# mLSTM layer with modulated norms: input projection in two passes over its rows, attention spread over the V and O strips

## The reference, cut to what matters

```
sh1, sc1, g1, sh2, sc2, g2 = split(silu(c) @ w_mod + b_mod, 6)       # w_mod 2048 x 12288
hm = rms_norm(x) * (1 + sc1) + sh1
q, k, v, o, g = split(hm @ w_in)                                     # 1024, 1024, 2048, 2048, 16 columns
h  = causal mLSTM of q, k, v with gates from g; per-head rms_norm * h_norm
x  = x + g1 * ((sigmoid(o) * h) @ w_out)
hf = rms_norm(x) * (1 + sc2) + sh2
x  = x + g2 * (conv_ffn(hf, w_up, conv, w_down))
```

## Time and profile before

| | us |
|---|---|
| median of 3 runs (1316.69 to 1318.73) | 1316.71 |
| span of the profiled execution, first to last instruction | 1314.5 |
| PE busy in it | 1190.8 (91%) |
| DVE busy | 942.9 (72%) |
| ACT busy | 552.2 (42%) |
| POOL busy | 202.8 (15%) |

### The profile page before, as it was taken

The page is one execution under the profiler, slowest core; times in us unless marked ns, Lnnn a source line. Parts: engine busy times, 40 slices in busy tenths (PEclk is TensorE's granted clock), DMA queues, the critical chain, the costliest instruction groups (busy, mean ns, idle before and its releaser), DMA issues.

```text
span 1314.5 us, 22606 instructions
## 1 busy us (share of the span) xinstructions
PE 1190.8 (91%) x8034; PEld 1104.8 (84%) x8034; DVE 942.9 (72%) x916; ACT 552.2 (42%) x711; POOL 202.8 (15%) x182
## 2 busy tenths in 40 slices
PE   0128998999999999499999999999999999999998
PEld 0127887999999888499999888999999888999986
DVE  7889883666667699779888756667666556776763
ACT  0315445444444444444444433444444434444432
POOL 0040000011010121212211112122111112222221
PEclk9958999999999999699999999999999999999999
DMA  8997997788687599759999556666665656666562
GB/s 360 422 401 284 407 362 203 199 246 226 192 236 246 195 364 369 221 166 270 271 283 286 193 194 194 189 178 175 189 191 177 204 190 179 181 186 175 179 197 90
DMA packets 303757, 311.24 MB, mean 237 GB/s; under 512 B 5000, under 2 KB 251208, under 8 KB 291176
## 3 DMA queue, kind: packets, MB, share of 16 engines
q1 hardware_dynamic: 303108, 310.42, 73.6%
q0 software_dynamic: 176, 0.16, 0.1%
q10 hardware_dynamic: 438, 0.19, 0.1%
HBM read 308.66 MB, written 2.10 MB: 236 GB/s over the span
## 4 chain that ended last, share of the span: by engine, by line
PE 86%; DVE 8%; issue 3%; DMA 2%; ACT 1%; POOL 1%; POOLq 0%; DVEq 0%; SPq 0%
PE ps L992 17%; PE ps L994 17%; PE ps L993 17%; PE ps L1012 10%; PE ps L1013 10%; PE ps L1014 10%; DVE acc L778 5%; DMA raw<-in_l_w_mod_dram 2%; PE ps L1021 1%; DVE hm_lo L764 1%; ACT w_hi L488 1%; DVE xnT L760 1%; DVE h_tok L870 1%; PE ps L1128 0%; PE ps L1125 0%
## 5 line engine op out<-in xcount | busy, mean ns | idle before, releaser
L741 DVE TENSOR_TENSOR w_lo<-raw,w_hi 128x1024 fp32r<-128x1024 f32 x392 | 520.0, 1340 | 214.0 <-ACT w_hi L488 214.0
L488 ACT ACTIVATE w_hi<-raw 128x1024 fp32r<-128x1024 f32 x392 | 414.0, 1057 | 400.6 <-PE ps L1014 228.2
L992 PE MATMUL ps<-hm_hi,w_hi 128*128 128x256 f32 x1920 | 546.9, 285 | 11.2 <-DVE hm_lo L764 9.1
L993 PE MATMUL ps<-hm_lo,w_hi 128*128 128x256 f32 x1920 | 544.5, 284 | 0.0
L994 PE MATMUL ps<-hm_hi,w_lo 128*128 128x256 f32 x1920 | 544.5, 284 | 0.0
L992 PEld LDWEIGHTS ps<-hm_hi,w_hi 128*128 128x128 f32 x1920 | 369.9, 193 | 11.6 <-issue 10.0
L993 PEld LDWEIGHTS ps<-hm_lo,w_hi 128*128 128x128 f32 x1920 | 370.0, 193 | 0.1
L994 PEld LDWEIGHTS ps<-hm_hi,w_lo 128*128 128x128 f32 x1920 | 369.8, 193 | 0.0
L753 DVE SCALAR_TENSOR_TENSOR acc<-mod_raw,cT,acc 128x2048 f32<-128x2048 f32 x64 | 151.1, 2362 | 7.7 <-DMA mod_raw<-in_l_w_mod_dram 7.6
L1012 PE MATMUL ps<-w_hi,act_hi 128*128 128x512 f32 x352 | 137.1, 389 | 0.0
L1013 PE MATMUL ps<-w_lo,act_hi 128*128 128x512 f32 x352 | 137.0, 389 | 0.0
(11 more groups left out here) (155 smaller groups left out, 1002.2 us busy)
## 6 DMA issues: line engine op xcount, KB each, us to landing
raw<-in_l_w_up_dram SPq DMA_DIRECT2D x88, 1024.0 KB, 5.8
mod_raw<-in_l_w_mod_dram SPq DMA_DIRECT2D x64, 1024.0 KB, 7.5
raw<-in_l_w_in_dram SPq DMA_DIRECT2D x48, 1024.0 KB, 7.9
raw<-in_l_w_down_dram SPq DMA_DIRECT2D x44, 1024.0 KB, 5.0
raw<-in_l_w_mod_dram SPq DMA_DIRECT2D x32, 1024.0 KB, 7.1
raw<-in_l_w_out_dram SPq DMA_DIRECT2D x16, 1024.0 KB, 7.5
x<-in_x_dram SPq DMA_DIRECT2D x2, 1024.0 KB, 10.0
out_dram<-x SPq DMA_DIRECT2D x8, 256.0 KB, 4.9
```

Source lines behind the costliest of these rows:

```text
L488: nc.scalar.activation(w_hi[:, v % 4, :], raw[:, v // 2 % 4, (v % 2) * HALF:(v % 2 + 1) * HALF], ACT.Copy).then_inc(w_hi_made, 1)
L741: nc.vector.tensor_tensor(w_lo[:, v % 4, :], raw[:, v // 2 % 4, (v % 2) * HALF:(v % 2 + 1) * HALF], w_hi[:, v % 4, :].bitcast(f32), ALU.su ...
L992: mm(out, hi, hm_hi[:, k, :], start=(k == 0), stop=False)
L993: mm(out, hi, hm_lo[:, k, :], start=False, stop=False)
```

## The change

It touches stages 1 to 7 up to the first up unit; the up and down products stay as they are.

**Prefix.** Scale and shift are first made for the first 768 columns only (`K_FIRST` = 6 row tiles). SP loads x and then 16 pieces `m0` of 256 rows x 768 columns, and these are summed by PE itself: `sum_m0` uses each 128x128 block of `m0` as stationary operand and one column of `cT` as the moving one. The remaining 1280 columns (`m1`, 32 pieces of 640 KB) are added up by DVE during the first pass.

**Input projection.** It runs over half units of two row tiles x 512 columns, `in_half`, in 12 strips (V0 to V3, O0 to O3, K0, K1, Q0, Q1). Pass 1 covers the first 6 row tiles (3 halves a strip, 36 in all). ACT stores the partial sums (`store_strip`). Pass 2 covers the other 10 (5 halves a strip, 60 in all): K and Q first, then V and O strips in turn. DVE adds the partial sums (`add_strip`). So K and Q of all heads exist before the attention.

**Attention.** The 40 V and O halves of pass 2 and the 32 halves of the output product are *slots*. In slot e each engine runs its split or its half and then `attend(e)`, which holds the pieces of a head at fixed slots: scores at 5+5h, product with V at 9+5h, transpose at 13+5h. `o_sig` and `gated` are now token-major and `o_lo` is made by DVE. x is overwritten by attention buffers and loaded again before the residual add.

**The other w_mod pieces.** A table, `MOD_SLOT`, gives the half after whose split DVE adds each piece.

```diff
+    K_FIRST = 6
+    PAIRS = (K_FIRST // 2, (KT - K_FIRST) // 2)
...
+    MOD_SLOT = [V_PASS1 + p for p in (6, 7, 9, 11, 12, 14, 16, 17, 19)] \
+        + [V_VO + e for e in (1, 3, 4, 8, 9, 11, 13, 14, 18, 19, 21, 23, 24, 28, 29, 31, 33, 34, 38, 39)] \
+        + [V_OUT + f for f in (3, 6, 8, 9, 11, 12, 13, 15, 17, 18, 19, 20, 21, 22, 23, 25, 27, 29, 30)]
...
+    E_SCORES, E_PV, E_HT, E_HEAD = 5, 9, 13, 5
...
             sp.dma_start(c_rows[:], c_d[0, :].rearrange("(k p) -> k p", p=P)).then_inc(c_in, 16)
-
-            for n in range(2):
-                sp.wait_ge(acc_cleared, n + 1)
...
+            for t in range(TB):
+                sp.dma_start(x[:, t, :], x_d[0, t * P:(t + 1) * P, :]).then_inc(x_in[t], 16)
+            for i in range(16):
+                load_m0(i)
+            for vh in range(6):
+                load_half(vh)
+            for i in range(2 * KT):
+                load_m1(i)
+                load_half(6 + i)
...
+                if r == 10:
+                    sp.wait_ge(hT_ready, H)
+                    for t in range(TB):
+                        sp.dma_start(x[:, t, :], x_d[0, t * P:(t + 1) * P, :]).then_inc(x_in[t], 16)
...
+            def sum_m0(i):
+                n, rt = i // 8, 2 * (i % 8)
+                pe.wait_ge(m0_in[i % 8], 16 * (n + 1))
+                for j in range(2):
+                    for k in range(K_FIRST):
+                        c0 = k * (KT + 1) + rt + j
+                        last = mm(ps[:, M0_BANK[n], c0:c0 + 1],
+                                  m0[:, i % 8, j * M0_COLS + k * P:j * M0_COLS + (k + 1) * P],
+                                  cT[:, rt + j:rt + j + 1], start=True, stop=True)
+                last.then_inc(m0_used, 1)
...
+            for p in range(V_PASS1):
+                in_half(p)
+                if p == 24:
+                    pe.wait_ge(m1_used, KT)
+                    pe.wait_ge(sc0_made, 2)
+                    column_sums(0, 3, 0, KT - K_FIRST)
+                if p == V_PASS1 - 3:
+                    pe.wait_ge(m1_used, 2 * KT)
+                    column_sums(1, 0, 0, KT - K_FIRST)
...
+            for p in range(V_PASS1):
+                split_lo(p + 3)
+                if 1 <= p <= 2 * KT:
+                    add_m1(p - 1)
```

More of the change, by code:

```diff
@@ L458, in _ @@
             rstd_of_x(1)
+            pool.wait_ge(colsum_done, 3)
             clear_acc(5)
@@ L654, in _, with store_strip @@
-            nc.scalar.preload_act_table_set("exp_and_others")
-            with act.Fori(0, H - 1) as h:
-                head(h, False)
-            head(H - 1, True)
-            nc.scalar.preload_act_table_set("silu_and_others")
+                    nc.scalar.activation(out, src, ACT.Copy, bias=1.0).then_inc(sc_made, 1)
+                else:
+                    nc.scalar.activation(out, src, ACT.Copy).then_inc(sc_made, 1)
+            def store_strip(m):
+                for b in range(2):
+                    nc.scalar.activation(strip_sums(0, m)[b], bank_pair(m, b), ACT.Copy)\
+                             .then_inc(evac0, 1)
@@ L661, in squares @@
+            for p in range(V_VO, V_OUT):
+                slot_hi(p)
+                attend(p - V_VO)
             def squares(q):
@@ L883, in _ @@
-            with dve.Fori(0, H - 1) as h:
-                head(h, False)
-            head(H - 1, True)
+            copy_xT(0)
+            for n, out in ((0, scale_p), (1, shift_p)):
+                dve.wait_ge(m0_summed, n + 1)
+                sums = ps[:, M0_BANK[n], 0:K_FIRST * (KT + 1)]
+                nc.vector.reduce_sum(out[:, 0:K_FIRST], sums.rearrange("p (b r) -> p b r", r=KT + 1),
+                                     mybir.AxisListType.X).then_inc(sc0_made if n else sc0_step, 1)
+                if n == 0:
+                    dve.wait_ge(sc0_step, 1)
+                    nc.vector.tensor_scalar(out[:, 0:K_FIRST], out[:, 0:K_FIRST], 1.0, None, ALU.add)\
+                             .then_inc(sc0_made, 1)
@@ L1149, in _ @@
-            with pe.Fori(0, H - 1) as h:
-                head(h, False)
-            head(H - 1, True)
+            for i in range(4, 16):
+                sum_m0(i)
+            for p in range(V_PASS1):
+                in_half(p)
[6 more added lines that the diff above has]
+                    column_sums(1, 0, 0, KT - K_FIRST)
@@ new lines, in _ @@
+            for p in range(V_PASS1, V_VO):
+                in_half(p)
+            pe.wait_ge(wg_made, 4)
+            pe.wait_ge(hm_made, KT)
+            pe.wait_ge(params_made, 3)
+            out = ps[0:F_ROW0 + H, 2, 0:SEQ]
+            for k in range(KT):
+                c0 = k // 8 * 2 * F_ROW0 + k % 8 * H
+                hi, lo = wg_hi[:, c0:c0 + F_ROW0 + H], wg_lo[:, c0:c0 + F_ROW0 + H]
+                mm(out, hi, hm_hi[:, k, :], start=(k == 0), stop=False)
+                mm(out, hi, hm_lo[:, k, :], start=False, stop=False)
+                last = mm(out, lo, hm_hi[:, k, :], start=False, stop=(k == KT - 1))
```

1042 lines of the change are left out of this document (567 added, 475 removed).

## The result

| | before | after |
|---|---|---|
| median of 5 runs each, in turn on one chip | 1318.73 us | 1326.61 us |
| lowest | 1316.69 | 1324.86 |
| profiled execution: span | 1314.5 | 1323.0 (its own time 1324.86) |

The ratio is 1.0063, with a 95% interval of 1.0045 to 1.0081: 0.6% slower. One run of after took 1402.14 us at a granted clock of 0.827, and is left out of the ratio; the others are at 0.954 to 0.956.

A forecast was written before the change was run, and what follows sets the result against it. Before the change: w_mod loads bound the prefix, then PE; after it, DVE sets the pace. Output product ending +10.4 and second norm -3.9 give +6.5 on 1314.5, so 1321; with run offset 1323 us, range 1300 to 1337.

The forecast's parts named there:

- step 1: Prefix: sums on PE at 0.216 us a record, 88.1 us; first half at 105.5 against 106.7, a gain of 1 us.
- Rival B: Prefix: the sums run at the full clock and lose 42 us, giving 1281 us; chance 0.10.
- steps 2 and 3: Pass 1, then K, Q and gates of pass 2: paced by PE, ending at 211.9 and 275.3, DVE's work hidden.
- step 4: V and O strips of pass 2: DVE 17.8 us plus 1.6 lost with ACT, 19.4 a head; slot 39 left at 427.3.
- So the order decides: V and O strips: DVE at 17.8 and PE at 18.2 us a head are level, so waits between engines set the pace.
- step 5: Output product: DVE is the path, 106 us plus 4 for loads, so 110; end at 537.3 where before 526.9.
- step 6: Second norm: both `add_mod` are gone from it, 33.8 - 3.9 = 29.9 us.
- my two gains: Second norm: 1.9 us as ready squares no longer wait for DVE, 2.0 from the add before the copies of the transposes.
- Rival C: Strips and output product: DVE not pinned to ACT, PE stays the bound; 22 to 24 us less, 1300; chance 0.20.
- D: Loads fall behind in pass 1, early pass 2 and the output product: +8 to +15 us, 1331 to 1338; chance 0.20.

## Why the prediction was right, and where it was not

1323 was forecast and 1326.6 measured, on the forecast side. DVE's work and its waits for loads are the path in the output product, nearly as forecast, and the loss arises there. But the terms of the strips and of the output product were each wrong by about as much as the result is large, and they cancelled: that the number came so near is luck.

**Prefix** (step 1): right. 0.214 us a record for my 0.216, sums ended at 99.6 for 101.5, first half at 103.65 for 105.5. In three other profiled executions with this prefix it starts at 106.9 to 107.0, so the 1.9 us on the good side are chance. Rival B fell, as it was argued against: the clock stays at 0.50 under one-column matmuls. The rule of the Trainium skill, "TensorE: Matmul & The Clock Gate", section "Why this matters for your kernels", that keeping TensorE continuously busy gets the full clock, does not hold for this work: 60.00:80.00 has PE busy for 20.00 of 20.00 us at 0.50. What I failed to ask was whether the sums belonged on PE at all: DVE was idle, and the sums on it are worth 43.4 us. The forecast took the change as given, and so its largest cost stood in it as a plain term.

**Passes 1 and 2, K and Q** (steps 2 and 3): right but for one term. PE full from 110 to 276, end of the gates at 276.4 for 275.3. DVE waited 5.9 us in 20 places for `m1` in pass 1, and PE stayed full. The stretch took 172.7 us for 169.8. What I had at nothing is the clock behind the column sums inside pass 1:
```profile
173.88 2.29 PE L1143 MATMUL ps<-ones,acc 128*128 128x1 f32 x20
...
176.56 0.41 PE L1135 MATMUL ps<-hm_hi,w_lo 128*128 128x256 f32 x1
```
Such a matmul has a record of 0.28 us ahead of them. The granted clock is 0.91 from 170 to 190 and 0.92 from 190 to 212, where the second sums stand: some 1.8 us lost each time, with PE full.

**Strips** (step 4): the step that failed. "So the order decides", and 19.4 us a head with PE waiting; measured are 17.8 to 18.0 with PE full, and without 2.1 us of each add the same. DVE left slot 39 at 418.7, not 427.3: 8.6 us too much. Two things were wrong in it. First, 17.8 of DVE work a head was too high (310 to 418 has 96.8 us busy in six heads, 16.1): I added up durations, but the next instruction starts before the record of the last one ends. The durations do add up to 107 us, 17.8 a head; the overlaps, 1.7 a head, are the difference. The rows of the longest wait above show two of them: a split that starts at 471.98 and has 1.22 is followed at 473.12, so its pace is 1.14; an add has 2.27 at 2.35. Second, the waits for ACT are real and of the size forecast (DVE stood 10.5 us for `w_hi` between 310 and 418, 1.75 a head for 1.6), but PE had split halves in hand and was full throughout; a wait of an engine with slack is no term of the sum. The first ten slots ended at 310.4 for 311.3, 34.0 us for 36.

**Output product** (step 5): "4" for DMA waits; measured 13.8. I had counted bandwidth, bytes a slot against the time of a slot, and not the round trip that two buffers allow: a piece is asked for when the second before it is done. Four buffers took all of it: 105.3 us from slot 39 to the last scaling (421.3 to 526.59), where I had 106 without the waits. The other terms were near: 19 adds 48 us for 44.6 (those beside POOL's adds took 3.36 instead of 2.34), waits for ACT 7.5 for 4.4, splits 42 for 44.7; here too the records overlap, so these add up to more than they take. 117.8 us instead of 110.

**Second norm** (step 6): 33.4 instead of 29.9. Of my two gains the first came: from the last scaling to the reduction of the squares there are 5.7 us for 7.6. The second, 2.0 for the add that stood before the copies, was not there to be had. In the kernel before that add had held the transposes up by 0.29 us only:
```profile
542.01 1.50 PE L1051 MATMUL ps<-ident,xn 128*128 128x128 f32 x12 [0.29 <-DVE xnT L924]
```
and in the changed kernel the transposes and column sums took 1.5 us more, not less:
```profile
545.71 6.54 PE L1165 MATMUL ps<-ident,xn 128*128 128x128 f32 x32 [14.18 <-DVE xn L1002]
552.08 4.18 PE L1143 MATMUL ps<-ones,acc 128*128 128x1 f32 x32
```
That is 10.55 us for 9.04: the clock rose 5.8 us into them (0.72 from 551 to 552), where before it rose 2.9 us into them (0.79 from 540 to 542).

**Sum**, measured against forecast: up to the gates +1.1 (276.4 for 275.3: prefix -1.9, passes +2.9), strips -9.7, output product +7.8, norm +3.5, the rest -0.8: together +2.0, and +6.5 became +8.5. The other 1.4 us between 1323 and 1326.6 are that the median of after lies 3.6 above its profiled span, where I took 2.2. Rival C was right of the strips, 142.3 us for its 141, though not by its own sign (DVE's waits for ACT under 0.5 us a head: they were 1.75); D was right of what DVE waits for in the output product; either alone would have been the worse forecast, since each was one of two errors that nearly cancel.

The prediction called itself wrong in sign "if the head cycle is under 18.5 us". The cycle was under it, and the sign held, because the output product took back what the strips gave.

## What to carry to other kernels

Before pricing a step that an engine now does, ask which idle engine could do it: 82 us of one-column matmuls were 35 us of adds and 10 of the small matmuls left. Where two engines are level, take the work of one away in a run and look at the cycle; a busy share of 95% does not name the bound. Price a double-buffered stream by its round trip (last read, request, landing behind what is already queued) and not by its bytes alone, and look for bursts such as a reload in that queue.

## What the runs showed of the hardware

- With one matmul of 256 columns to three of one column the clock stayed at 1.00 from 52 to 111 us, behind the transposes; at 0.50, the same mix did not raise it in 65 us. It fell right behind 12 one-row matmuls of 1.5 us, and not where three wide ones stood among them. It fell as well behind 20 column-sum records of 2.29 us in the midst of wide matmuls (0.91 from 170 to 190).
- The clock column reads 1.00 up to the first change of the clock in a trace, also where the durations (0.214 us a record) are those of the low level. In a prefix the durations are to be trusted.
- An add of 2048 columns beside POOL's adds to x took 3.36 us instead of 2.34, a split 2.04 instead of 1.22. The Trainium skill, "SBUF — State Buffer", section "Who interferes with whom", says that a DVE instruction with two inputs in SBUF contends with a GpSimd instruction that reads SBUF. The trace agrees: both of these have two such inputs, and they lost 1.0 and 0.8 us.
